# Backward direction on off-diagonal quarters, merged tiles taken singly, second down unit early: one layer of a hybrid attention/RWKV-7 backbone

## The reference

```python
def _wkv7_scan(r, w, k, v, kk, a, s0, reverse):
    def step(s, inp):
        r_t, w_t, k_t, v_t, kk_t, a_t = inp
        sa = jnp.einsum("bhvk,bhk->bhv", s, -kk_t)
        s = (s * w_t[:, :, None, :] + sa[..., None] * (kk_t * a_t)[:, :, None, :]
             + v_t[..., None] * k_t[:, :, None, :])
        return s, jnp.einsum("bhvk,bhk->bhv", s, r_t)
    ...
# _rwkv7_bidir: for d, reverse in enumerate((False, True)): one scan forward, one backward, y = ys[0] + ys[1]
# _layer:
    merged = (jax.nn.sigmoid(ga) * (attn_o @ p["w_attn_br"])
              + jax.nn.sigmoid(gr) * (rwkv_o @ p["w_rwkv_br"]))
    x = x + gate1[:, None, :] * (merged @ p["w_out"])
    h2 = _modulate(_rmsnorm(x, p["norm2_g"]), shift2, scale2)
    up = _dwconv3(h2 @ p["ffn_up"], p["ffn_conv"])
    up_u, up_g = jnp.split(up, 2, axis=-1)
    x = x + gate2[:, None, :] * ((jax.nn.silu(up_g) * up_u) @ p["ffn_down"])
```

## Time and profile before

| | us |
|---|---|
| median of 3 runs (lowest, highest) | 1376.88 (1375.66, 1378.38) |
| the profiled execution | 1380.84 |
| its span, first to last instruction | 1379.1 |
| mean granted TensorE clock | 0.977 |
| PE busy | 1294.0 (94%) |
| VectorE busy | 689.9 (50%) |
| ScalarE busy | 550.1 (40%) |
| chain that ended last: PE | 60% |
| PE at L712 (dense products) / L1206 (down) / L882 and L870 (G, H), share of the chain | 30% / 11% / 2% and 2% |

### The profile page before, as it was taken

The page is one execution under the profiler, slowest core; times in us unless marked ns, Lnnn a source line. Parts: engine busy times, 40 slices in busy tenths (PEclk is TensorE's granted clock), DMA queues, the critical chain, the costliest instruction groups (busy, mean ns, idle before and its releaser), DMA issues.

```text
span 1379.1 us, 31730 instructions
## 1 busy us (share of the span) xinstructions
PE 1294.0 (94%) x13903; PEld 1196.7 (87%) x13903; DVE 689.9 (50%) x1036; ACT 550.1 (40%) x864; POOL 42.1 (3%) x103
## 2 busy tenths in 40 slices
PE   4899999998999769899999899899999999899996
PEld 1899999997999545499989788799999999899995
DVE  3437642642544676565556412654545545434544
ACT  4645534422233477533342121733334333233433
POOL 0100011000010000010000000000000000000000
PEclk9999999999999998999999999999999999999998
DMA  9322365315000200011017574021221211022222
GB/s 389 143 71 102 110 271 180 105 45 209 8 5 4 92 1 1 0 53 34 8 41 259 225 294 177 31 88 65 64 88 61 91 61 46 23 66 71 69 76 92
DMA packets 24027, 131.70 MB, mean 96 GB/s; under 512 B 2896, under 2 KB 3664, under 8 KB 15344
## 3 DMA queue, kind: packets, MB, share of 16 engines
q1 hardware_dynamic: 19104, 103.98, 21.5%
q0 software_dynamic: 4816, 26.11, 5.0%
HBM read 111.74 MB, written 18.34 MB: 94 GB/s over the span
## 4 chain that ended last, share of the span: by engine, by line
PE 60%; DVE 3%; ACT 2%; issue 1%; DVEq 0%; ACTq 0%
PE ps L712 30%; PE ps L1206 11%; PE ps L882 2%; PE ps L870 2%; PE ps L1093 1%; PE ps L850 1%; PE ps L737 1%; PE ps L756 1%; PE ps L1069 1%; PE ps L999 1%; PE ps L747 1%; DVE nmax L1972 1%; PE ps L1070 1%; PE ps L862 1%; PE ps L1040 1%
## 5 line engine op out<-in xcount | busy, mean ns | idle before, releaser
L712 PE MATMUL ps<-h2lo,whi 128*128 128x322 f32 x672 | 154.5, 311 | 0.7 <-ACT facc L1308 0.7
L712 PE MATMUL ps<-h2hi,wlo 128*128 128x322 f32 x672 | 155.0, 312 | 0.0
L712 PE MATMUL ps<-h2hi,whi 128*128 128x322 f32 x672 | 154.0, 310 | 0.0
L1662 DVE TENSOR_TENSOR wlo<-raw,whi 128x2048 fp32r<-128x2048 f32 x47 | 107.5, 2288 | 70.4 <-ACT whi L1269 70.4
L712 PE MATMUL ps<-hlo,whi 128*128 128x322 f32 x544 | 127.9, 316 | 1.0 <-ACT qkv L1334 1.0
L712 PE MATMUL ps<-hhi,wlo 128*128 128x322 f32 x544 | 125.4, 312 | 0.0
L712 PE MATMUL ps<-hhi,whi 128*128 128x322 f32 x544 | 124.7, 310 | 0.0
L712 PEld LDWEIGHTS ps<-h2hi,whi 128*128 128x128 f32 x672 | 114.2, 190 | 0.0
L712 PEld LDWEIGHTS ps<-h2lo,whi 128*128 128x128 f32 x672 | 113.0, 189 | 0.9 <-DVE wlo L1662 0.9
L712 PEld LDWEIGHTS ps<-h2hi,wlo 128*128 128x128 f32 x672 | 113.6, 189 | 0.0
L1709 DVE SCALAR_TENSOR_TENSOR facc<-fraw,par,facc 128x642 f32<-128x642 f32 x44 | 39.0, 887 | 138.7 <-ACT facc L1308 138.7
(11 more groups left out here) (339 smaller groups left out, 2596.7 us busy)
## 6 DMA issues: line engine op xcount, KB each, us to landing
raw<-in_wblk SPq DMA_DIRECT2D x48, 1024.0 KB, 4.9
adl<-in_wada SPq DMA_DIRECT2D x8, 2048.0 KB, 7.9
raw<-in_wdn SPq DMA_DIRECT2D x44, 256.0 KB, 2.6
adaw<-in_wada SPq DMA_DIRECT2D x4, 2048.0 KB, 20.7
gate_scratch<-gout POOLq DMA_DIRECT2D x16, 322.0 KB, 2.5
gld<-gate_scratch POOLq DMA_DIRECT2D x8, 644.0 KB, 4.6
attention_inputs_used<-attention_scratch SPq DMA_DIRECT2D x1, 5056.0 KB, 15.5
u_scratch<-uout POOLq DMA_DIRECT2D x12, 320.0 KB, 2.4
```

The lines of the kernel that those rows point to most:

```text
L712: mm = pe.matmul(o, w, v, start=first, stop=last and w is hi and x is xh[n])
L1662: TT(wlo[s][:, :], raw[s][:, :], whi[s][:, :].bitcast(F32), ALU.subtract).then_inc(lo_done, 1)
```

## The change

Four edits.

1. H, G1 to G4, P and U: the backward direction's products (d = 1) go to the array's two off-diagonal quarters. H and P write the result of head r to the other head's 64 partitions (`away`), into the next bank; G1 to G4, U bring it back. For that, `rm` has a third plane: plane 2 holds the backward direction's R in the other half. R0 fills it with two more predicated copies; V is now three transposes (two of half the partitions that cross over into plane 2, one of the forward direction); V5 merges into planes 0 and 2. G5 reads planes 0 and 2 and writes on the diagonal. The loops run q outside and d inside, so four different quarters follow one another. Waits that change: H1 waits for AK in place of T0 (it writes the bank that AK reads); P0 takes over Y0's wait for the last Y1; the last P1 also waits for its own engine's Y0. POOL's preset writes six planes in place of four. Buffers `smid` move.
2. Output projection: the first output tile is computed merged tile by merged tile, each on its own low part; `ada_late(4)` moves to just before the eighth.
3. Down projection: unit 1 gets operand buffers of its own (`dhi_second`, `dlo_second`, and the upper half of `whi[0]`, `wlo[0]`) and is prepared right after unit 0, ahead of the last up block.
4. The waits of ScalarE that go with it.

```diff
-        rm[s] += [sb(f"rm{s}_{g}", [P, 2, 2, CH]) for g in range(2)]
+        rm[s] += [sb(f"rm{s}_{g}", [P, 3, 2, CH]) for g in range(2)]
...
+    dhi_second, dlo_second = (sb(name, [P, TP - 2], F32R) for name in ("dhi_second", "dlo_second"))
...
-                               i64.unsqueeze(1).broadcast_to([P, 4, CH])).then_inc(po_g[s], 1)
+                               i64.unsqueeze(1).broadcast_to([P, 6, CH])).then_inc(po_g[s], 1)
...
-                dv("T0" if l == 1 else f"C{l - 1}")
-                for d in range(2):
-                    for q in range(2):
-                        for r in half:
-                            mm = pe.matmul(bank(b1, CH, CH * (2 * d + q))[r], abm[s][g % 2][r, d, q, 0, :], tm[s][r, d, q, :],
-                                           start=True, stop=True)
+                dv("AK" if l == 1 else f"C{l - 1}")
+                for q in range(2):
+                    for d in range(2):
+                        for r, away in zip(half, half[::-1]):
+                            mm = pe.matmul(bank(b0 + d, CH, CH * q)[away if d else r], abm[s][g % 2][r, d, q, 0, :],
+                                           tm[s][r, d, q, :], start=True, stop=True)
...
+                        for r, away in zip(half, half[::-1]):
+                            at = away if d else r
+                            turned, right = rm[s][g % 2][at, 2 * d, q, :], hm[s][at, d, q, :]
                             if l == 5:
+                                mm = pe.matmul(bank(b0, CH, 4 * CH + CH * (2 * d + q))[at], right, turned, start=True, stop=True)
+                            else:
+                                mm = pe.matmul(bank(b0 + d, CH, 2 * CH + CH * q)[r], turned, right, start=True, stop=True)
...
                 if q == 0:
                     ac("TR")
+                    if g > 0:
+                        if g - 1 in ADDED:
+                            dv("Y1", g - 1)
+                        else:
+                            ac("Y1", g - 1)
...
                 else:
                     dv("S0")
+                    if g == NG - 1:
+                        pe.wait_ge(pe_g[s], at_stage(PE_ST, it, g, "Y0"))
+                for n in range(1 if first else 2):
+                    for d in range(2):
+                        for r, away in zip(half, half[::-1]):
+                            left, right = (ar[s][r, d, chunk_of(g, d, q), 0, :], state(q)[r, d, :]) if n else \
+                                (akm[s][g % 2][r, d, q, 0, :], vt64[s][r, chunk_of(g, d, q), :])
+                            mm = pe.matmul(bank(b2 + d, CH, 6 * CH)[away if d else r], left, right, start=n == 0,
+                                           stop=first or n == 1)
...
+                        at = away if d else r
+                        mm = pe.matmul(bank(b2 + d, CH, 7 * CH)[r], rm[s][g % 2][at, 2 * d, q, :], pw[s][at, d, :], start=True,
+                                       stop=True)
...
-        pe.wait_ge(tile_evac, 2 * BLK_OUT + 2)
-        ada_late(4)
-        pe.wait_ge(m_lo, KD)
+        def out_first():
+            pe.wait_ge(lo_done, BLK_OUT + 1)
+            pe.wait_ge(hi_done, BLK_OUT + 1)
+            pe.wait_ge(tile_evac, 2 * BLK_OUT + 1)
+            for k in range(KD):
+                if k == KD - 1:
+                    pe.wait_ge(tile_evac, 2 * BLK_OUT + 2)
+                    ada_late(4)
+                pe.wait_ge(m_lo, k + 1)
+                hi, lo = (w[BLK_OUT % 2][:, k * 256:k * 256 + P] for w in (whi, wlo))
+                for q, (w, x) in enumerate(((hi, mlo[k]), (lo, mhi[k]), (hi, mhi[k]))):
+                    for o, v in zip(out_halves(0), halves(x)):
+                        mm = pe.matmul(o, w, v, start=k == 0 and q == 0, stop=k == KD - 1 and q == 2)
+            mm.then_inc(tile_done, 1)
...
         up_block(NBLK - 2, FF - 2, 0, False, False)
-        ac.wait_ge(act_done, 1)
+        ac.wait_ge(act_done, 2)
         ac.wait_ge(tile_done, 2 * NBLK - 2)
         down_hi(0, 0, 0, True)
+        down_hi(1, 1, 1, True)
         up_block(NBLK - 1, FF - 1, 1, False, False)
-
         ac.wait_ge(act_done, FF)
-        ac.wait_ge(tile_done, 2 * NBLK)
-        down_hi(1, 1, 1, True)
...
-                ins = dv.copy_predicated(r1[:, :, :, :], near.unsqueeze(2).broadcast_to(each), steps_of(bank(b1))[:, :, :, 0:CH])
+                made = steps_of(bank(b1))[:, :, :, 0:CH]
+                ins = dv.copy_predicated(r1[:, 0:2, :, :], near.unsqueeze(2).broadcast_to(each), made)
+                for r, away in zip(half, half[::-1]):
+                    ins = dv.copy_predicated(r1[away, 2, :, :], near[r, 1].unsqueeze(1).broadcast_to([CH, 2, CH]), made[r, 1])
...
-                src, dst = (r1, t1) if name == "T0" else (t1, r1)
-                ins = dv.transpose(dst[:, :, :, :].rearrange("p d q n -> p (d q n)"), src[:, :, :, :].rearrange("p d q n -> p (d q n)"))
+                if name == "T0":
+                    ins = dv.transpose(t1[:, :, :, :].rearrange("p d q n -> p (d q n)"),
+                                       r1[:, 0:2, :, :].rearrange("p d q n -> p (d q n)"))
+                else:
+                    for r, away in zip(half, half[::-1]):
+                        dv.transpose(r1[away, 2, :, :].rearrange("p q n -> p (q n)"), t1[r, 1, :, :].rearrange("p q n -> p (q n)"))
+                    ins = dv.transpose(r1[:, 0, :, :].rearrange("p q n -> p (q n)"), t1[:, 0, :, :].rearrange("p q n -> p (q n)"))
```

More of the change, by code:

```diff
@@ L891, in chunk_stage @@
                     dv("S0")
[L892 to L897, removed]
-                            mm = pe.matmul(bank(b2, CH, CH * d)[r], ar[s][r, d, chunk_of(g, d, q), 0, :], state(q)[r, d, :],
-                                           start=False, stop=True)
+                    if g == NG - 1:
+                        pe.wait_ge(pe_g[s], at_stage(PE_ST, it, g, "Y0"))
+                for n in range(1 if first else 2):
+                    for d in range(2):
+                        for r, away in zip(half, half[::-1]):
[3 more added lines that the diff above has]
+                                           stop=first or n == 1)
             elif name[0] == "U":
@@ L904, in chunk_stage @@
                 for d in range(2):
-                    for r in half:
-                        mm = pe.matmul(bank(b2, CH, P + CH * d)[r], rm[s][g % 2][r, d, q, :], pw[s][r, d, :], start=True, stop=True)
+                    for r, away in zip(half, half[::-1]):
+                        at = away if d else r
+                        mm = pe.matmul(bank(b2 + d, CH, 7 * CH)[r], rm[s][g % 2][at, 2 * d, q, :], pw[s][at, d, :], start=True,
+                                       stop=True)
             elif name[0] == "S":
@@ L1194, in down_unit @@
         def down_unit(n, s, k, again=False):
+            second = k == 1 and n == 1
             pe.wait_ge(d_hi, n + 1)
             pe.wait_ge(d_lo, n + 1)
+            xh, xl = (dhi_second, dlo_second) if second else (dhi[s], dlo[s])
             for f in (2, 3, 0, 1) if k == 0 and not again else range(4):
-                hi, lo = whi[s][:, f * P:f * P + P], wlo[s][:, f * P:f * P + P]
+                at = (4 + f if second else f) * P
+                hi, lo = (w[0 if second else s][:, at:at + P] for w in (whi, wlo))
                 outs = out_halves(2 * f, TP - 2)
@@ L1604, in down_hi @@
                 ac.wait_ge(d_used, n - 1)
[L1605 to L1606 removed]
+            second = first and s == 1
+            ac.activation(whi[0][:, 512:1024] if second else whi[s][:, 0:512], raw[s][:, 0:512], ACT.Copy)
+            ac.activation((dhi_second if second else dhi[s])[:, :], af[:, k, :], ACT.Copy).then_inc(d_hi, 1)
         up_block(NBLK - 2, FF - 2, 0, False, False)
[L1609 removed]
+        ac.wait_ge(act_done, 2)
         ac.wait_ge(tile_done, 2 * NBLK - 2)
         down_hi(0, 0, 0, True)
+        down_hi(1, 1, 1, True)
         up_block(NBLK - 1, FF - 1, 1, False, False)
         ac.wait_ge(act_done, FF)
[L1615 to L1616 removed]
         for g in range(2):
@@ L1832, in chunk_stage @@
             r1, t1 = rm[s][g % 2], tm[s]
+            half = [slice(64 * h, 64 * h + 64) for h in range(2)]
             def mine(n):
```

52 lines of the change are left out of this document (26 added, 26 removed).

## The result

The changed kernel takes 1390.8 us (median of 6 runs, 1389.8 to 1394.0) against 1377.75 before (6 runs, 1375.7 to 1383.6): a ratio of 1.0091, 95% interval 1.0074 to 1.0108. It is slower by 13 us where the forecast was 9.6 faster, and outside the range. Its profiled execution has a span of 1390.1 us.

What follows compares the result with a forecast made beforehand. TensorE's time was taken as the round's time, with VectorE alternating and uncovered by shorter TensorE work. Passes +2.8, merged tiles -5.9, down unit -6.5 gave -9.6: 1376.9 to 1367.3 us, range 1357 to 1379.

Steps and rivals of the forecast that it cites:

- Part 2: VectorE in the two chunk passes: 5.9 us more VectorE a round; walked through the rounds, +2.8 us for both passes.
- TensorE's half time: Passes: four quarters side by side halve H, G1 to G4, P and U, freeing 5.6 us of TensorE a round.
- The third rival: Passes: the four quarters don't work side by side, TensorE keeps 23.1 us a round; 1389 us; chance 0.08.
- VectorE's prices: V and R0: 0.30 us per short instruction without overlap, so V 0.90 us a stream and R0 1.07.
- Rivals 1 and 2: Passes: short VectorE instructions cost nearly what long ones do, 1383.7 us, chance 0.12; or they overlap, 1351.7 us, chance 0.12.
- rival 1: V and R0: short instructions cost nearly what long ones do, making VectorE the wall; 1383.7 us; chance 0.12.
- H1's wait: Head of a steady round: TensorE idle from 3.96 us after KB, ended by AK; H1 at 6.13, before 4.43.
- The steady round: Passes: later H1 offset by shorter stages behind it, -0.4 us in sum, rounds of 23.5 us.
- The first round: First round of a pass: H1 +2.4, three level periods +1.3, end -0.3; +3.4 us, to 20.5.
- Last round: Last round of a pass and its lagged rest: P and U alone halve, -1.2 us.
- the fourth rival: Passes: more idle time drops TensorE's clock to 1.2 GHz; four falls of 3.4 us, 1374.1 us; chance 0.08.
- The parts outside: Outside the passes: merged tiles singly -5.9 us, second down unit early -6.5 us.

Runs made afterwards that it cites:

- e1: The quarters and VectorE's turning alone on the kernel before, merged tiles and down units as before: 1400.2 us, ratio 1.0142.
- e5: Changed kernel plus products nobody reads in TensorE's waits: 32 before H1 in rounds 2 to 5, 4 before each H2-H5, G1-G4 of the first round: 1386.8 us.
- e2: Merged tiles singly and second down unit early, without the quarters, on the kernel before: 1369.4 us, ratio 0.9941.
- e12: e2 measured again, beside later kernels: 1370.0 us, ratio 0.9938 to the kernel before.
- e11: Changed kernel with H1 and G1 on two quarters, no R0 copies, H1 not waiting for AK; V1 to V4 turn R: 1361.6 us.
- e7: Changed kernel with four quarters only for H5, P, U; only V4 turns R, no R0 copies, H1 not waiting for AK: 1361.8 us.
- e10: Changed kernel with four quarters only for H4, G4, H5, P, U; V3, V4 turn R, no R0 copies, H1 not waiting for AK: 1361.1 us.
- e4: Changed kernel plus products nobody reads in TensorE's waits: 48 before H1 in rounds 2 to 5, 10 before each H2-H5, G1-G4 of the first round: 1406.0 us.
- e6: e2 with the adaLN block moved from before k = 7 to before k = 3 of the first output tile: 1375.8 us, ratio 0.9977.

## Why the prediction was wrong

**The step that failed** is the price of the passes, Part 2 with its walk: "One pass: 3.4 - 0.8 - 1.2 = +1.4 us, two passes +2.8". They cost 16.6 in the traces, 22 as e1. The durations in it were right; what they do to TensorE was not. In pass 1, which cost 8.9 us for 1.4 forecast, the first round took 7.1 us more than before (forecast 3.4), the second 1.6 (0), the third 0.3 (-0.4), the fourth 0.6 less (-0.4; the kernel before took 24.8 there), the last with its rest 0.4 more (-1.2). In pass 0 the second, third and fourth took 1.4, 2.4 and 2.5 more, and the first only 1.1, since a long pause of the kernel before is not in it (last section).

- *TensorE's half time*: right. H of both streams takes 0.47 us against 0.93 in the earlier trace rows, and TensorE's busy time fell by 23 us. The third rival, taken from the Trainium skill, "TensorE: Matmul & The Clock Gate", section "Part 3: Packing small matmuls — row/col tiling", is out: products on the diagonal and the off-diagonal quarters of the same rows do run side by side, 16 records (eight products) in 0.23 us.
- *VectorE's prices*: right within 0.02 us (0.306, 0.312 and 0.297 against 0.30). V is 0.98 us a stream, with 0.015 between instructions and no overlap, as the Trainium skill, "VectorE: DVE Perf Modes", section "Two Vector instructions with no wait between them", has it and as the casts of the earlier trace rows had it. Rivals 1 and 2 are out by their condition, the price of an instruction. What rival 1 is headed by, VectorE as the wall, came true all the same, at R0 and at 0.30 us each: its run of eleven stands on the chain.
- *H1's wait*: foreseen at 2.17 us and ended by AK, and it is just that. H1 began 6.30 us after KB, forecast 6.13.
- *The steady round*: forecast 23.5, it is 24.15 at full clock. H2 to G3 took 4.7 us instead of 4.2 (V at 0.98, a wait of 0.38 us for U's copy that I had not in the walk), H5 and G5 2.5 instead of 2.16. So the wait ahead of H1 was not given back.
- *The first round*: forecast 20.5; 24.2 in pass 1, at a mean clock of 0.65. e5's, with the clock mostly at full, is 22.3 with some filler in it. So some 2 us of the 3.7 missing are the clock's, and the rest is not told apart.
- *Last round*: forecast -1.2, it was +0.4 in each pass. P, ScalarE's copy, U, copy, S and Y follow one another there; the halved products only lengthen the waits for the copies.
- *The clock*: the fourth rival had the mechanism and a third of its size: four falls of 3.4 us are 13.6 us at the low level, and there were 41 more than before (47.8 against 6.8), most of them in the first rounds. Of its two readings, the first (a mean clock of 0.90 in a first round) holds, and the second was wrong. The window of 495 to 505 us with TensorE busy 4.65 of 10 was taken as a sign that a half idle TensorE keeps its clock, at 0.95. It ends 0.9 us into a fall, which follows that stretch at once and lasts to 510.9. The trace before, cut at that place:

```profile
495.00:504.10 9.10, 4.65 (x20) 3.24 (x20) 5.79 (x10) 8.08 (x15) 0.00 (x0) 1.00 0.00 1
504.10:510.90 6.80, 5.54 (x18) 4.51 (x19) 1.92 (x2) 4.96 (x11) 0.00 (x0) 0.50 0.01 2
```

  The forecast's own walk had the hole in every round: 2.2 us before H1 with TensorE at some 80%. Each round was a chance for a fall, and I counted two a pass; one fell in nearly every steady round of pass 0.
- *The parts outside*: merged tiles -4.0 for -5.9, the down unit -5.9 for -6.5, both in the forecast's direction; as kernels of their own -8.8 (e2) and -9.7 (e12), for -12.4. The 1.9 missing at the first junction are the adaLN load, whose cover I put at 3 us with "up to 1 us is lost"; it lost 1.6 to 1.9.

What stood for the wrong net was the belief that a hole in front is paid back by shorter stages behind. The shorter stages are real, but smaller than forecast, and not all where the walk had them. In e11's fourth round of pass 1 (22.3 us, against 23.8 of a steady round in e12), H2 to G3 takes 4.6 us instead of 5.4, a saving of 0.8 where 1.08 was forecast, and e7, with P and U alone, has 0.55 of it. H4 and G4 take 1.8 instead of 2.1, where 0.40 was forecast. Another 0.7 is saved ahead of S0, where the walk lost 1.08. In the changed kernel H2 to G3 gains the same 0.7 and H4 and G4 0.5, and S0 begins 1.4 us later than before: the hole at H1 costs what they gain, and the clock comes on top.

## What to carry to other kernels

Ask of an added VectorE instruction what TensorE has to do meanwhile, not how long it lasts: 1.2 us of short copies ahead of the first H of a round, which put it off by 1.65, cost 20.8 us in ten rounds; 4.5 us a round in stages further on cost 5.6. Count with it the overlap that its neighbours lose. A trick that speeds one engine by loading another is best applied stage by stage, only where the load has cover, as in e7, e10 and e11; count a new idle hole of some 2 us in every round as a risk to TensorE's clock, and not only as its length. And a transfer that is moved must be checked against the one it will then run beside.

## What the hardware showed that was not expected

*Pauses of TensorE without a releaser.* With the products in quarters, or filler among them, TensorE stands still for 0.4 to 1.5 us at places where it waits for no other engine; the profile calls them "issue". e12 has next to none in its steady rounds, e4 has 1.9 us of them in one. The queue that brings instructions moved in 16 KB packets, and these are its rows in the DMA view of e4's round from 657.4 (25.8 us) and of e12's from 626.3 (23.8 us):

```profile
q8 instruction: 7, 0.11, 2.1%
```

```profile
q8 instruction: 5, 0.08, 1.4%
```

That is a packet every 3.7 us and one every 4.8. In the first round of pass 0, with the DMA engines 77% busy, one such pause lasted 5.14 us in the kernel before and 2.95 in e12:

```profile
342.13 1.76 PE L870 MATMUL ps<-tm,abm 64*64 64x64 f32 x28 [5.14 <-issue]
```

```profile
341.39 1.76 PE L873 MATMUL ps<-tm,abm 64*64 64x64 f32 x28 [2.95 <-issue]
```

The first round of pass 0 has the same instructions in the kernel before, e2, e6 and e12, and takes 25.1, 21.8, 25.1 and 22.9 us, with the long pause at 5.14, 2.67, 5.14 and 2.95. In all four traces an instruction packet lands shortly before that pause ends, and TensorE goes on 1.3 to 1.5 us after the landing (340.82 and 342.13 in the kernel before, 339.90 and 341.39 in e12); so it does after the shorter pause of the same round, and after the 0.86 us in e4 above (670.84 and 672.19). It fits instructions arriving late, and it is 2 to 3 us by which kernels differ without their edits; no run isolates it, so the cause is argued and not shown.

*The clock.* A steady round of the changed kernel was granted 1.00 in pass 1, with TensorE busy 19.8 of 24.2 us, and 0.94 in pass 0 with the same instructions, and e1's rounds of the same make had a fall in each. e7's rounds, busy 22.35 of 22.6, had none.
